# Two fused transformer blocks: shared offsets of operands in 2 KB, a first x block and weight piece in halves, and other fillers

## What is computed

```python
def first_block(x, ...):            # differential attention (4 heads) and two-way retention (4 heads)
    xn = _rms(x, norm_w)
    h = xn @ w_in                   # [512, 1024] x [1024, 3584]
    qa, ka, va, ga, qr, kr, vr, gr = split(h)
    oa = rms(softmax1(qa ka) va - lam * softmax2(qa ka) va) ; orr = rms(retention(qr, kr, vr))
    x = x + concat(oa * silu(ga), orr * silu(gr)) @ w_out

def second_block(x, ...):           # gated convolution beside windowed attention with 4 KV heads
    u = _rms(x, norm_g) @ w_in_2    # [1024, 8704]
    v_c, b_c, c_c, z_c, q, k, v, z_a, gate_logits = split(u)
    y_a = (b_c * conv3(c_c * v_c) * silu(z_c)) @ w_conv_out
    y_b = (window_attention(rms(q), rms(k), v) * silu(z_a)) @ w_attn_out
    ga, gb = split(sigmoid(gate_logits + gate_b))
    x = x + (ga * y_a + gb * y_b) @ w_out_2
```

## Time and profile before

| what | value |
|---|---|
| median of three runs | 827.24 us (825.78 to 829.4) |
| the profiled execution | 829.72 us |
| its span, from first to last instruction | 827.8 us |
| around the span | 1.92 us |
| mean granted clock of TensorE | 0.997 |

### The profile page before, as it was taken

One profiled execution on the slowest core, in us unless ns is written; L12 is line 12 of the kernel. 1 busy time (PEld: TensorE's weight loads), 2 busy tenths in 40 slices (PEclk: granted clock), 3 DMA queues, 4 the chain that ended last, 5 costly groups with the idle time before them and its releaser, 6 DMA issues.

```text
span 827.8 us, 11437 instructions
## 1 busy us (share of the span) xinstructions
PE 818.5 (99%) x4230; PEld 690.9 (83%) x4230; DVE 611.6 (74%) x1094; ACT 321.3 (39%) x701; POOL 182.2 (22%) x188
## 2 busy tenths in 40 slices
PE   9999999999999999999999998999999999999998
PEld 7788788888888888888888887888888888999986
DVE  4898777769984476785579787887952259499998
ACT  3464475632112254344445444541001112355580
POOL 3112111111121211121334435444222223000000
PEclk9999999999999999999999999999999999999999
DMA  7232214445142222653255554556876235766562
GB/s 237 76 103 77 77 52 151 152 156 178 52 178 94 85 79 77 201 178 94 85 128 127 128 128 102 127 128 135 167 180 153 82 96 153 211 189 186 179 203 77
DMA packets 128461, 108.92 MB, mean 132 GB/s; under 512 B 4445, under 2 KB 100758, under 8 KB 128406
## 3 DMA queue, kind: packets, MB, share of 16 engines
q1 hardware_dynamic: 121510, 93.50, 36.9%
q0 software_dynamic: 6336, 12.58, 9.2%
q10 hardware_dynamic: 560, 2.11, 0.7%
HBM read 106.08 MB, written 27.26 MB: 161 GB/s over the span
## 4 chain that ended last, share of the span: by engine, by line
PE 86%; DVE 6%; ACT 4%; issue 2%; POOL 1%; DMA 0%; DVEq 0%; ACTq 0%; POOLq 0%
PE proj L1690 22%; PE proj L1688 22%; PE proj L1689 22%; PE bank_t L1702 3%; PE bank_o L1773 2%; PE score L1689 1%; PE score L1690 1%; PE score L1688 1%; ACT prob L1047 1%; PE score L1759 1%; PE score L1758 1%; PE proj L1907 1%; DVE w_lo L1113 1%; DVE acc L1255 1%; PE bank_o L1690 1%
## 5 line engine op out<-in xcount | busy, mean ns | idle before, releaser
L1113 DVE TENSOR_TENSOR w_lo<-w_raw,w_hi 128x1024 fp32r<-128x1024 f32 x146 | 185.6, 1274 | 68.5 <-POOL w_hi L697 67.9
L697 POOL TENSOR_SCALAR w_hi<-w_raw 128x1024 fp32r<-128x1024 f32 x110 | 130.3, 1185 | 452.5 <-DMA w_raw<-in_w_in_dram 331.3
L1688 PE MATMUL proj<-xt_hi,w_hi 128*128 128x512 f32 (+1 forms) x448 | 171.4, 383 | 0.0
L1690 PE MATMUL proj<-xt_hi,w_lo 128*128 128x512 f32 (+1 forms) x448 | 168.4, 376 | 0.0
L1689 PE MATMUL proj<-xt_lo,w_hi 128*128 128x512 f32 (+1 forms) x448 | 168.0, 375 | 0.0
L1690 PEld LDWEIGHTS proj<-xt_hi,w_lo 128*128 128x128 f32 x448 | 84.5, 189 | 15.7
L1689 PEld LDWEIGHTS proj<-xt_lo,w_hi 128*128 128x128 f32 x448 | 84.7, 189 | 14.4
L1688 PEld LDWEIGHTS proj<-xt_hi,w_hi 128*128 128x128 f32 x448 | 84.6, 189 | 14.1
L1688 PE MATMUL proj<-w_hi,xt_hi 128*128 128x512 f32 x152 | 60.9, 401 | 0.3 <-ACT prob L889 0.3
L1690 PE MATMUL proj<-w_hi,xt_lo 128*128 128x512 f32 x152 | 59.6, 392 | 0.0
L1689 PE MATMUL proj<-w_lo,xt_hi 128*128 128x512 f32 x152 | 59.4, 391 | 0.0
(11 more groups left out here) (415 smaller groups left out, 1778.0 us busy)
## 6 DMA issues: line engine op xcount, KB each, us to landing
w_raw<-in_w_in_dram SPq DMA_DIRECT2D x80, 512.0 KB, 3.7
w_sums<-in_w_in_dram SPq DMA_DIRECT2D x8, 1024.0 KB, 7.6
w_raw<-w_sums SPq DMA_DIRECT2D x32, 256.0 KB, 3.2
w_raw<-in_w_out_dram SPq DMA_DIRECT2D x14, 512.0 KB, 3.3
w_sums<-w_sums POOLq DMA_DIRECT2D x6, 1024.0 KB, 10.2
w_raw<-in_w_in_dram SPq DMA_DIRECT2D x24, 256.0 KB, 3.3
w_sums<-in_w_out_dram SPq DMA_DIRECT2D x4, 1024.0 KB, 7.2
w_sums<-in_w_in_dram POOLq DMA_DIRECT2D x4, 1024.0 KB, 9.9
```

The source lines that it names most:

```text
L697: pool.tensor_scalar(hi, raw, 1.0, 1.0, ALU.mult, ALU.mult).then_inc(hi_done, 1)
L1113: dve.tensor_tensor(lo, raw, hi.bitcast(F32), ALU.subtract).then_inc(w_split, 1)
L1688: pe.matmul(out, left[0], right[0], start=first, stop=False)
L1690: return pe.matmul(out, left[1], right[0], start=False, stop=last)
```

## The change

Twenty small tensors that only the first block uses move to the end of stack `one`, the mask (1 KB) to the end of stack `two`, and 32 unused values are declared behind the last small tensor. The mask is made in GpSimd's order behind the rounding that follows piece 40, no longer at the start. x's first block and the first weight piece are each loaded in two halves, in turns, with semaphores of their own; GpSimd, VectorE and TensorE take piece 0 by halves; XT 1 moves behind the first four matmuls of piece 0. The fillers are no longer 18 transposes of 128 columns but 3 and 1 float32 matmuls of 256 columns on a tensor that VectorE clears first; they no longer wait for ident.

```diff
-        mask = sb("mask", [P, 2 * P])
...
-        lam_s = sb("lam_s", [P, 2]); lam_e = sb("lam_e", [P, 2]); neg_lam = sb("neg_lam", [P, 1])
...
+        to_whole_rows = sb("to_whole_rows", [P, 32])
...
+        lam_s = sb("lam_s", [P, 2], stack=one); lam_e = sb("lam_e", [P, 2], stack=one); neg_lam = sb("neg_lam", [P, 1], stack=one)
...
+        mask = sb("mask", [P, 2 * P], stack=two)
...
-            for i in range(4):
+            for c, x_arrived, w_arrived in ((0, x_first, raw_first), (1, x_landed[0], raw_landed[0])):
+                sp.dma_start(x_in[:, :, c * P:(c + 1) * P],
+                             a["x"][0, :, c * P:(c + 1) * P].rearrange("(s p) c -> p s c", p=P)).then_inc(x_arrived, 16)
+                sp.dma_start(w_raw[:, 0, 512 * c:512 * c + 512], a["w_in"][0, c * P:(c + 1) * P, 512:1024]).then_inc(w_arrived, 16)
+            for i in range(1, 4):
...
+            def prepare_mask():
+
+                pool.wait_ge(piece_done, 4 * U_KV)
+                pool.memset(mask[:], 0.0).then_inc(pool_chain, 1)
...
-            for n in range(SLOTS - 1):
+            pool.wait_ge(raw_first, 16)
+            pool.tensor_scalar(w_hi[:, 0, 0:512], w_raw[:, 0, 0:512], 1.0, 1.0, ALU.mult, ALU.mult).then_inc(hi_first, 1)
+            pool.wait_ge(raw_landed[0], 16)
+            pool.tensor_scalar(w_hi[:, 0, 512:D], w_raw[:, 0, 512:D], 1.0, 1.0, ALU.mult, ALU.mult).then_inc(hi_done, 1)
+            for n in range(1, SLOTS - 1):
                 round_piece(n)
...
+                if n == 4 * U_Q20:
+                    prepare_mask()
...
+            dve.memset(sq[:], 0.0).then_inc(warm_ready, 1)
             dve.wait_ge(norms_turned, 1)
             dve.tensor_copy(norm_cols[:], bank_t[:, 0:2 * KC]).then_inc(norms_ready, 1)
             dve.wait_ge(norms_ready, 1)
-            split_piece(0)
+            dve.wait_ge(hi_first, 1)
+            dve.tensor_tensor(w_lo[:, 0, 0:512], w_raw[:, 0, 0:512], w_hi[:, 0, 0:512].bitcast(F32), ALU.subtract).then_inc(first_split, 1)
             take_xt_low(0)
+            dve.wait_ge(hi_done, 1)
+            dve.tensor_tensor(w_lo[:, 0, 512:D], w_raw[:, 0, 512:D], w_hi[:, 0, 512:D].bitcast(F32), ALU.subtract).then_inc(w_split, 1)
             take_xt_low(1)
...
                 for _ in range(count):
-                    pe.transpose(bank(U_K, 3)[:, 0:P], ident[:], ident[:])
-
+                    pe.matmul(bank(U_K, 3)[:, 0:256], sq[:, 0:P], sq[:, 0:256], start=True, stop=True)
+
+            pe.wait_ge(warm_ready, 1)
+            keep_busy(3)
             pe.wait_ge(setup, 1)
-            keep_busy(10)
             step("XT", 0)
-            keep_busy(4)
             pe.wait_ge(norms_landed, 32)
             pe.transpose(bank_t[:, 0:2 * KC], norm_rows[:], ident[0:2 * KC, 0:2 * KC]).then_inc(norms_turned, 1)
-            step("XT", 1)
-            keep_busy(4)
+            keep_busy(1)
...
                                 if l == r:
-                                    pe.wait_ge(hi_done, 1)
+                                    pe.wait_ge((hi_first, hi_done)[kk], 1)
                                     pe.wait_ge(xt_hi_done, kk + 1)
                                 elif l:
                                     pe.wait_ge(xt_split, kk + 1)
                                 else:
-                                    pe.wait_ge(w_split, 1)
+                                    pe.wait_ge((first_split, w_split)[kk], 1)
...
+                                if kk + l + r == 0:
+                                    step("XT", 1)
```

More of the change, by code:

```diff
@@ L313, in build @@
         rs_v = sb("rs_v", [P, 32]); rs_y = sb("rs_y", [P, 32]); rs_t = sb("rs_t", [P, 32])
-        mx = sb("mx", [P, 2, 2]); neg_mx = sb("neg_mx", [P, 2, 2]); den = sb("den", [P, 2, 2])
-        rec = sb("rec", [P, 8, 2]); lam_rec = sb("lam_rec", [P, 2, 1])
         mx2 = sb("mx2", [P, 4, 4]); neg_m2 = sb("neg_m2", [P, 4, 4]); sink_m = sb("sink_m", [P, 4, 4])
         den2 = sb("den2", [P, 4, 4]); sink_e = sb("sink_e", [P, 4, 4]); rec2 = sb("rec2", [P, 4, 4])
+        to_whole_rows = sb("to_whole_rows", [P, 32])
         conv_w = cols[:, 0:R_GATE].rearrange("p (k t) -> p k t", k=3)
@@ L359, in build @@
         dmat = sb("dmat", [P, RET_HEADS, P], stack=one)
+        lam_s = sb("lam_s", [P, 2], stack=one); lam_e = sb("lam_e", [P, 2], stack=one); neg_lam = sb("neg_lam", [P, 1], stack=one)
+        first_use = sb("first_use", [P, 1], stack=one)
+        lam_j = sb("lam_j", [P, HD], stack=one)
+        dec = sb("dec", [P, 8], stack=one); dec_a = sb("dec_a", [P, 8], stack=one); dec_e = sb("dec_e", [P, 8], stack=one)
+        dec_z = sb("dec_z", [P, 8], stack=one); dec_q = sb("dec_q", [P, 8], stack=one); dec_p = sb("dec_p", [P, 8], stack=one)
+        log_g = sb("log_g", [P, 8], stack=one); steps_to = sb("steps_to", [P, 4], stack=one)
+        ret_c = sb("ret_c", [P, 6, RET_HEADS], stack=one); rs_k = sb("rs_k", [P, ST], stack=one)
+        neg_log_b = sb("neg_log_b", [P, 4], stack=one)
+        mx = sb("mx", [P, 2, 2], stack=one); neg_mx = sb("neg_mx", [P, 2, 2], stack=one); den = sb("den", [P, 2, 2], stack=one)
+        rec = sb("rec", [P, 8, 2], stack=one); lam_rec = sb("lam_rec", [P, 2, 1], stack=one)
         one.close()
@@ L521, in build @@
         x_landed = [sem(f"x_landed{s}") for s in range(ST)]
+        x_first = sem("x_first"); raw_first = sem("raw_first"); hi_first = sem("hi_first"); first_split = sem("first_split")
+        warm_ready = sem("warm_ready")
         x_again = sem("x_again")
@@ L682, in _ @@
             pool.iota(table[:, 0, :].bitcast(I32), pattern=[[1, TAB]], base=-CENTRE, channel_multiplier=-1).then_inc(setup, 1)
[L684 to L690, removed]
+            def prepare_mask():
+                pool.wait_ge(piece_done, 4 * U_KV)
+                pool.memset(mask[:], 0.0).then_inc(pool_chain, 1)
+                pool.wait_ge(pool_chain, 2)
+                pool.affine_select(out=mask[:], in_=mask[:], compare_op=ALU.is_ge, fill=BIG, base=P,
+                                   pattern=[[-1, 2 * P]], channel_multiplier=1).then_inc(pool_chain, 1)
+                pool.wait_ge(pool_chain, 3)
+                pool.affine_select(out=mask[:], in_=mask[:], compare_op=ALU.is_ge, fill=BIG, base=-1,
+                                   pattern=[[1, 2 * P]], channel_multiplier=-1).then_inc(setup_mask, 1)
             def round_piece(n):
@@ L773, in row_squares @@
             def row_squares(s):
+                act.wait_ge(x_first, 16)
                 for i in range(4):
@@ L1714, in step @@
                             wait_evacuated(pe, U_O0 + c // 4, s)
-                    if b == 0 and c % 2 == 0:
+                    if m == 0:
+                        pe.wait_ge(x_first, 16)
+                    elif m == 1:
+                        pe.wait_ge(x_landed[0], 16)
+                    elif b == 0 and c % 2 == 0:
                         pe.wait_ge(x_landed[c // 2], 16)
```

## The result

The changed kernel takes 822.08 us (median of 16 runs, 821.53 to 825.62), the kernel before 827.37 in the same comparison (16 runs, 825.78 to 829.99). The ratio is 0.9943, with a 95% interval of 0.9931 to 0.9955: 5.3 us are won where 7.2 were forecast. The profiled execution takes 821.56 us, its span is 819.5, the mean granted clock 1.000.

A forecast was written before the change was run, and what follows sets the result against it. TensorE, busy in 99% of the span, was taken as the bound. Offsets (2.6 + 2.6 + 0.3 - 0.3 = 5.2) plus start (2.0) gave 7.2 us, so 827.24 became 820.0 us, range 816.8 to 824.2.

The forecast's parts named there:

- Offsets, 512 columns: Attention and convolution units: shared offsets speed matmul starts, 2.6 us in five mix/yc units, 2.6 us in four unbroken ones.
- it is the difference that counts, not the 128: Matmul spacing throughout: slow where the two operands' offsets in 2 KB differ, 233.3 against 226.7 ns at 512 columns.
- offsets don't matter: Rival for the whole kernel: offsets bring nothing or aren't shared, only the start gains, 825.2 us; chance 0.13.
- Gate products: Matmuls of 256 columns: eight of 28 products may lose by equal offsets, -0.3 us (-0.6 to 0).
- Final product: Last product: six of 14 pieces mixed, 0.08 us each; only the four behind the s_lo wait count, 0.3 us.
- The start up to piece 1: Kernel start: first real matmul at 6.0 to 6.4 us, piece 0 done at 13.9 instead of 16.13; 2.0 us taken.
- these had not raised the clock: Kernel start: transposes from 1.59 us left the clock low; it rose only after 2 to 3 us of matmuls proper.
- The following pieces are far from their data: After piece 0: weight piece 1 and x's next blocks arrive well before needed, so the start's 2.0 us stays in the sum.
- The parameters that move ... cost nothing: the same instructions at other addresses: Small tensors moved into the first phase's memory: no cost, 0 us in the sum.
- the clock stays low: Rival for the start: clock low to 10.6 us, so the start wins 0.5 and the kernel takes 821.5 us; chance 0.20.
- More gain: Rival: units U_RQK to U_GR become regular, another 1.5 us, and no accident 1 to 2 more: 817 us; chance 0.12.
- Slower by accidents: Rival, windowed attention 403 to 560 us: more collisions of GpSimd's masking and VectorE's split, 3.9 us each; chance 0.05.

The follow-up runs named there:

- start_only: Changed kernel with 504 unused values in place of 32, putting x_in and all behind it back to offset 2016: 827.42 us, ratio 0.9991 to the kernel before.
- shift_128: Changed kernel with 32 more unused values, moving x_in and all behind it 128 bytes against the weight rings: 826.99 us, one run.
- shift_256: Changed kernel with 64 more unused values, moving x_in and all behind it 256 bytes against the weight rings: 824.67 us, one run.
- old_fillers: Changed kernel with ten and four transposes of ident as fillers again, in place of 3 and 1 matmuls: 825.65 us, one run.
- layout_only: Changed kernel with the start of the kernel before; only the memory map and the mask's place are new: 824.43 us, ratio 0.9954 to the kernel before.
- layout_series: New memory map with the old start, reciprocal-root chain half a piece later and decay series moved to 76 and 84 us: 825.13 us, ratio 0.9959 to before.
- rs_later: Changed kernel with VectorE's reciprocal-root chain hooked half a piece later, behind the awaited xt_lo: 822.48 us, ratio 0.9929 to the kernel before.
- series_later: Changed kernel with the reciprocal-root chain half a piece later and the decay series moved behind steps at 76 and 84 us: 821.38 us, ratio 0.9916 to before.
- after_again: The changed kernel itself, unaltered, measured again in another comparison: 822.83 us, ratio 0.9934 to the kernel before.
- shift_32: Changed kernel with 8 more unused values, moving x_in and all behind it 32 bytes against the weight rings: 825.62 us, one run.
- three_edits: Changed kernel with reciprocal-root chain and decay series later, sx moved 32 bytes, all behind it 512, and piece 71 split earlier: 820.28 us, ratio 0.9906 to before.

## Why the prediction was right, and where not

- **Offsets, 512 columns.** Right, and nearly to size: 2.40 of 2.6 us in the five units with mix and yc, 2.57 of 2.6 in the four unbroken ones. start_only undoes it with nothing but 1,888 bytes of unused memory. The step "it is the difference that counts, not the 128" holds too, but within 256 bytes and not within 2 KB: the kernel before had only the offsets 128 and 2016 to show, and these differ under either reading.
- **Rival "offsets don't matter".** Refuted. The Trainium skill, "SBUF — State Buffer", Who interferes with whom, gives TensorE two independent read ports for moving and weights and says that it never waits on anyone. By that rule shift_128 and shift_256 should be alike; their units take 22.40 and 21.76 us. These rows show that the pair of addresses matters; what in the engine makes it matter, no run here shows.
- **Gate products.** The sign was right, the loss 0.42 in place of 0.3 us: all 28 went to 2.88, so more than half of the possible 0.6 was lost. That only these eight could lose was right, but not for the reason of unequal offsets alone: the products of sx with ring one were unequal too and stood at 2.88 already.
- **Final product.** -0.23 of -0.3. Piece 7 gives 0.22 back waiting for s_lo, as the step said it would, and the end of the kernel 0.3 more, since VectorE now runs last. That the tail's chain would pass to VectorE altogether I had not said.
- **The start up to piece 1.** Forecast 6.0 to 6.4 and 13.9, measured 6.28 and 13.69. The sizes are right and one reason is wrong: "these had not raised the clock". Transposes can, as old_fillers and layout_only show, and the new fillers' part in the gain is not shown by any run. The Trainium skill, "TensorE: Matmul & The Clock Gate", Part 4: PE-mode transpose, says that the high clock does not engage for transposes, as they don't count as busy in the same way. Here no such rule can be read off: 1.16 and 1.15 us for the first four matmuls after transposes speak against it, layout_series' 1.65 and the 2.06 of before for it, and the same code of TensorE gave both.
- **The start carried to the end.** This is the step that failed: "The following pieces are far from their data". I looked at weight pieces and at x's blocks and found each early, and did not look at VectorE, busy 8.31 of the 9 us from 26 to 35 in the kernel before. Of 2.44 us at piece 1, 0.84 are left at U_Q. rs_later moved the wait instead of removing it, and series_later, which took 3.5 us off VectorE besides, stood 1.14 us better than rs_later at U_V: that names VectorE's sum as a bound. The late landing of piece 4 (rounded at 20.56, before at 19.66) is in the same chain, for VectorE idled 2.02 us for it. rs_later and series_later keep it and lose the wait at 27, so it alone does not make the wait; what the start would have kept had piece 4 come in time was not tried.
- **"The parameters that move ... cost nothing: the same instructions at other addresses".** Not so, by the one profile of the kernel before: with the new map, piece 4 takes 5.5 us or more from issue to landing in place of 3.6. Which tensor's move does it, or whether the mask does, stays open.
- **The range.** It was said to cover the bounds of start and offsets, but the low ones together (2.0 and 0.5 us) give 824.7, above its end of 824.2. The 822.08 lies inside either way.
- **Rival "the clock stays low".** It foresaw about the measured time (821.5) by another way. The clock was high; the time went to VectorE.
- **More gain.** The units U_RQK to U_GR won 0.31 in U_RQK and little else, not 1.5.
- **Slower by accidents.** The accident did not multiply, but neither is it rarer in the changed kernel: 5 of 16 runs have the drop, 6 of 17 before. It is frequent with the new map and the old start (8 of 12) and absent from the 23 runs in the last row of the table, one of them the same kernel again. At C3 the 14 profiles part by the length of the wait: the four longest, 1.76 to 2.75 us, are followed by the drop, the ten of 1.15 to 1.71 are not. At 27 us no such order shows. The wait's length was not varied by itself, so that it decides is an argument. layout_only and after_again ran in one comparison, so chip and hour do not explain their difference; for the changed kernel's 5 of 16 against none of 5 in after_again they may.

## What to carry to other kernels

Lay tensors that meet in TensorE as moving and stationary operand so that their addresses agree within 256 bytes where matmuls have 512 columns; a declaration of unused values does it, and a stretch between starts shows it (21.76 or 22.40 us for 96 matmuls). Where they have 256 columns, try a distance (32 bytes brought 2.80 to 2.83 us in place of 2.88 here) and measure, since one of the unequal pairs was no faster. A gain early in a kernel is only kept if every engine behind it has room: before it is added to the sum, read the busy time of the helping engines over the following stretch, not only whether the next operand is there.

## What the runs showed of the hardware

- The offset's effect has a grain: shifts of 32 and 128 bytes cost the full 0.64 us per 96 matmuls of 512 columns, 256 and 512 nothing. For 256 columns it also matters which side lies where: 2.88 us for 24 with the moved operand at 2016 and the stationary one at 128, 2.81 to 2.85 the other way round. That shift_32 has its sx products with ring one at 2.80 us and three_edits, with sx and ring one at the same addresses, at 2.83 is not explained.
- The clock dropped to 0.50 behind waits of 1.65 us at 27 (old_fillers), 1.57 at 27.87 (shift_256) and of 1.76 to 2.75 at 496 to 500 (old_fillers, layout_series, before, layout_only), and not behind one of 1.65 at 27.89 (shift_128) or 1.71 at 495.61 (series_later). Each drop lasted 3.41 us, and the executions with one are 1.5 to 2.8 us longer in the medians above.
- A copy of four values a partition took 1.01 us on VectorE beside GpSimd's rounding and 0.16 us without it.
